# RMS norms of a two-block network on one core: first unit on unnormalized chunks, squares summed over chunks on VectorE, two norms in one pass

## What is computed

```python
def rms_norm(x, g, eps=NORM_EPS):
    xf = x.astype(jnp.float32)
    y = xf * lax.rsqrt(jnp.mean(xf * xf, axis=-1, keepdims=True) + eps)
    return (y * g.astype(jnp.float32)).astype(x.dtype)
```

## Time and profile before

| | |
|---|---|
| runs before | 2290.65, 2292.4, 2299.65 us; median 2292.4 |
| span of the profiled execution | 2289.6 us |
| the profiled execution's own time | not on the page; the median of the runs is 2.8 us above the span |
| TensorE matmul busy | 2172.8 us, 95% of the span |
| VectorE, ScalarE busy | 515.9 us (23%), 445.0 us (19%) |
| mean granted TensorE clock | 0.976 |
| memory traffic | 564 MB, 246 GB/s over the span |

### The profile page before, as it was taken

One profiled execution on the slowest core, in us unless ns is written; L12 is line 12 of the kernel. 1 busy time (PEld: TensorE's weight loads), 2 busy tenths in 40 slices (PEclk: granted clock), 3 DMA queues, 4 the chain that ended last, 5 costly groups with the idle time before them and its releaser, 6 DMA issues.

```text
span 2289.6 us, 27419 instructions
## 1 busy us (share of the span) xinstructions
PE 2172.8 (95%) x10542; PEld 1477.0 (65%) x10543; DVE 515.9 (23%) x1139; ACT 445.0 (19%) x794; POOL 6.9 (0%) x23
## 2 busy tenths in 40 slices
PE   8999989999999999999999899899999997999999
PEld 7686744444454444444444577678888886878887
DVE  3442111111121111111111128211000196110000
ACT  3342122222221221222222212221000123220000
POOL 0000000000000000000000000000000000000000
PEclk9999999999999999999999799999999998999999
DMA  7332679999999997999999633323444330324420
GB/s 298 124 134 92 241 298 422 422 422 422 422 371 356 422 402 299 421 422 422 422 422 422 249 111 111 146 75 147 155 158 147 128 130 32 116 74 147 149 90 19
DMA packets 78590, 564.36 MB, mean 246 GB/s; under 512 B 8864, under 2 KB 9248, under 8 KB 10176
## 3 DMA queue, kind: packets, MB, share of 16 engines
q1 hardware_dynamic: 77328, 554.94, 60.9%
q0 software_dynamic: 1200, 8.52, 0.9%
HBM read 558.19 MB, written 5.24 MB: 246 GB/s over the span
## 4 chain that ended last, share of the span: by engine, by line
PE 89%; DVE 5%; ACT 4%; issue 1%; DMA 0%; DVEq 0%; ACTq 0%; SPq 0%
PE bank L398 30%; PE bank L677 18%; PE bank L694 9%; PE bank L953 7%; PE bank L652 5%; DVE B L1775 3%; PE bank L704 3%; PE bank L520 2%; PE bank L726 2%; ACT B L997 2%; PE bank L408 2%; PE bank L745 1%; PE bank L664 1%; PE bank L643 1%; PE bank L903 1%
## 5 line engine op out<-in xcount | busy, mean ns | idle before, releaser
L398 PE MATMUL bank<-xn,ring 128*128 128x256 f32 x2560 | 574.2, 386 | 4.7 <-DVE xn L1338 4.7
L398 PEld LDWEIGHTS bank<-xn,ring 128*128 128x128 f32 x2560 | 495.5, 194 | 78.4 <-issue 9.2
L677 PE MATMUL bank<-ring,B 128*64 128x512 f32 x1920 | 418.6, 594 | 2.2 <-issue 2.2
L997 ACT ACTIVATE B<-bank 128x512 f32<-128x512 f32 (+3 forms) x293 | 150.0, 533 | 1279.2 <-PE bank L398 470.6
L677 PEld LDWEIGHTS bank<-ring,B 128*64 128x64 f32 x1920 | 135.5, 137 | 262.6 <-issue 259.0
L694 PE MATMUL bank<-ring,B 128*64 128x512 f32 x960 | 212.6, 595 | 0.0
L953 PE MATMUL bank<-B,ring 128*128 128x256 f32 x704 | 155.2, 379 | 0.0
L694 PEld LDWEIGHTS bank<-ring,B 128*64 128x64 f32 x960 | 66.3, 137 | 123.5 <-issue 119.9
L953 PEld LDWEIGHTS bank<-B,ring 128*128 128x128 f32 x704 | 133.8, 190 | 18.2
L652 PE MATMUL bank<-B 128*128 128x128 f32 x1056 | 124.7, 277 | 0.0
L398 PE MATMUL bank<-B,ring 128*128 128x256 f32 x512 | 116.2, 387 | 8.0 <-DVE B L1801 6.1
(11 more groups left out here) (266 smaller groups left out, 1442.9 us busy)
## 6 DMA issues: line engine op xcount, KB each, us to landing
ring<-in_stream SPq DMA_DIRECT2D x524, 1024.0 KB, 10.2
mem_kv<-ring POOLq DMA_DIRECT2D x4, 1024.0 KB, 7.2
B<-mem_kv POOLq DMA_DIRECT2D x4, 1024.0 KB, 6.8
xT<-in_x SPq DMA_DIRECT2D x1, 1024.0 KB, 4.9
ring<-in_mem SPq DMA_DIRECT2D x1, 1024.0 KB, 17.4
out_y<-xT SPq DMA_DIRECT2D x4, 256.0 KB, 2.5
tab<-in_tables SPq DMA_DIRECT2D x1, 960.0 KB, 10.6
tab<-in_tables SPq DMA_DIRECT2D x1, 544.0 KB, 11.5
```

Of the source, the lines that this page charges most:

```text
L398: mm = pe.matmul(dst[:, m, :], tile(u, m * C + k), rhs[:, k, :], start=(k == 0), stop=(k == C - 1))
L677: mm = pe.matmul(PS[4 + kind][NARROW * h:NARROW * (h + 1), :], xs[:, k, NARROW * h:NARROW * (h + 1)], ring[:, expert_slot(j), D * kk + 512 ...
L997: return act.activation(out_, in_, fn, **kw)
```

## The change

1. **Gains.** VectorE multiplies each residual chunk by the norm's gain alone into a new tensor xg, directly behind the residual add of its pair (gains).
2. **First unit on xg.** The first unit after a norm runs on xg instead of xn. Its output lacks the factor of each token; VectorE multiplies it in when it takes the bank out of PSUM (scale_first), into a new tensor un (or the tensor that ScalarE copied to before). The units behind the first still read xn, which is now xg x rb (normalize), two chunks in one operation, where rb is a copy of the spread in SBUF (copy_spread, ScalarE).
3. **Squares.** VectorE adds the pairs of squares into the first pair (add_squares, three operations of 128x512). TensorE then sums over the partitions with 4 matmuls (stat) instead of 16, placed inside the first unit behind its eighth matmul; the spread stands in front of its last one.
4. **Router.** Router and transposes read xg; the token's factor is applied by VectorE on the logits and by ScalarE on the token rows.
5. **Two norms in one pass.** For final and mix0 the product of both gains is applied at once. VectorE also sums squares weighted by the square of the final gain (in un); two more matmuls give the second mean of squares, from which the second factor is computed on 128x2 values. xT is multiplied by the final factor later, behind the scaling of the first units.
6. **Feed-forward ends.** The last down unit signals each bank (down_mm), and the residual adds start while it runs.
7. **Small ones.** Cross attention's query units use banks 0 and 1. Some semaphores are merged. The descriptor scratch of GpSimd's DMAs is set to 4096 (dynamic_dma_scratch_size).

The norms count 0 to 7 afterwards. The core of the diff:

```diff
@@ TensorE
-            def stationary(u, dst, rhs, ready=None):
+            def stationary(u, dst, rhs, ready=None, after=None):
...
-                            pe.wait_ge(ready[0], ready[1] + k + 1)
+                            pe.wait_ge(ready[0], ready[1] + k // ready[2] + 1)
...
+                        if after is not None and (m, k) in after:
+                            after[m, k]()
...
-                for c in (2 * j, 2 * j + 1):
+            def stat(n):
+                pe.wait_ge(S["ssum_ready"], n + 1)
+                for b in range(2):
+                    for c in range(2):
+                        mm = pe.matmul(PS[stat_bank(n)][:, b:b + 1], sq[:, c, b * P:(b + 1) * P], tb("ones")[:, 0:1],
+                                       start=(c == 0), stop=(c == 1))
+                if n == 2:
...
+                        mm = pe.matmul(PS[stat_bank(n)][:, 2 + b:3 + b], un[:, 0, b * P:(b + 1) * P],
+                                       tb("ones")[:, 0:1], start=True, stop=True)
+                mm.then_inc(S["stat_mm"], 1)
+            def spread(n):
+                pe.wait_ge(S["std_ready"], DEVS[n] + (4 if n == 2 else 2))
...
+            def first_unit(n, u, dst):
+                stationary(u, dst, xg, gained(n), {(0, 7): lambda: stat(n), (1, 6): lambda: spread(n)})
...
                 for j in range(4):
                     stationary(first + j, two(j), rhs, ready if j == 0 else None)
-                    if j and n is not None:
-                        stat_pair(n, j - 1)
-                if n is not None:
-                    stat_pair(n, 3)
...
-            for j in range(4):
-                stat_pair(0, j)
-            stationary(AT["lru_x"], two(0), xn, (S["xn_ready"], 0))
+            stationary(AT["lru_x"], two(0), xg, gained(0))
+            stat(0)
+            stationary(AT["lru_x"] + 1, two(1), xg, None, {(0, 7): lambda: spread(0)})
...
+            stat(1)
             for g in range(4):
...
-                                      xn[:, 4 * (g % 2) + c, (g // 2) * P:(g // 2 + 1) * P], tb("ident"))
+                                      xg[:, 4 * (g % 2) + c, (g // 2) * P:(g // 2 + 1) * P], tb("ident"))
...
-            for n in (2, 3):
-                for j in range(4):
-                    stat_pair(n, j)
-            for j in range(4):
-                stationary(AT["iq"] + j, two(j), xn, (S["xn_ready"], 24) if j == 0 else None)
+            stationary(AT["iq"], two(0), xg, gained(2), {(0, 7): lambda: stat(2)})
+            stationary(AT["iq"] + 1, two(1), xg, None, {(0, 1): lambda: spread(2)})
+            for j in range(2, 4):
+                stationary(AT["iq"] + j, two(j), xn, normed(2) if j == 2 else None)
...
+                    if g == NG - 1 and m % 2 and m < C - 1:
+                        mm.then_inc(S["down_mm"], 1)
...
@@ ScalarE
+            def copy_spread(n):
+                act.wait_ge(S["stat_mm"], STATS[n] + 2)
+                f(rb[:, :], PS[7 if n == 2 else stat_bank(n)][:, 0:T], ACT.Copy).then_inc(S["rb_ready"], 1)
...
-            for j in range(2):
-                act.wait_ge(S["units_done"], j + 1)
-                f(lxp[:, 2 * j:2 * j + 2, 2:2 + T], two(j), ACT.Copy).then_inc(S["lx_ready"], 1)
...
+            act.wait_ge(S["std_ready"], DEVS[1] + 2)
             for g in range(4):
                 act.wait_ge(S["tok_mm"], g + 1)
-                f(xtok[:, g // 2, 512 * (g % 2):512 * (g % 2) + 512], PS[6 + g % 2][:, :], ACT.Copy)\
+                f(xtok[:, g // 2, 512 * (g % 2):512 * (g % 2) + 512], PS[6 + g % 2][:, :], ACT.Identity,
+                  scale=nst[:, g // 2:g // 2 + 1])\
...
-            norm(2, "eps5")
-            norm(3)
+                squares(2, j)
+            deviation(2, "eps5")
+            act.wait_ge(S["std_ready"], DEVS[2] + 2)
+            f(nst2[:, :], nst2[:, :], ACT.Sqrt, scale=1.0 / D, bias=V("eps6")).then_inc(S["std_ready"], 1)
+            copy_spread(2)
...
@@ VectorE
+            def gains(n, j, gain):
...
+                for c in (2 * j, 2 * j + 1):
+                    g = gfm[:, c:c + 1] if n == 2 else V(gain, c)
+                    ts(xg[:, c, :], xT[:, c, :], g, None, ALU.mult).then_inc(S["xg_ready"], 1)
+            def add_squares(n, j):
+                dve.wait_ge(S["sq_ready"], 4 * n + j + 1)
+                settle()
+                if n == 2:
+                    for c in (2 * j, 2 * j + 1):
+                        if c == 0:
+                            link(ts(un[:, 0, :], sq[:, 0, :], gf2[:, 0:1], None, ALU.mult))
+                        else:
+                            link(stt(un[:, 0, :], sq[:, c, :], gf2[:, c:c + 1], un[:, 0, :], ALU.mult, ALU.add))
+                if j:
+                    o = tt(sq[:, 0:2, :], sq[:, 0:2, :], sq[:, 2 * j:2 * j + 2, :], ALU.add)
...
-                    stt(dst[:, k, :], xT[:, k, :], V(gain, k), PS[stat_bank(n)][:, 0:T], ALU.mult, ALU.mult)\
+            def normalize(n):
+                dve.wait_ge(S["xg_ready"], C * n + C)
+                dve.wait_ge(S["rb_ready"], SCALED[n] + 1)
+                for j in range(4):
+                    tt(xn[:, 2 * j:2 * j + 2, :], xg[:, 2 * j:2 * j + 2, :], over(rb[:, :], 2), ALU.mult)\
                         .then_inc(S["xn_ready"], 1)
-            def residual(first):
+            def scale_first(u, bank, dst, done):
+                dve.wait_ge(S["units_done"], u + 1)
+                tt(dst, two(bank), over(rb[:, :], 2), ALU.mult).then_inc(done, 1)
+            def norm(n, gain, u, bank):
+                rescale(n)
+                scale_first(u, bank, un[:, :, :], S["un_ready"])
+            def residual(first, n, gain):
                 for j in range(4):
                     dve.wait_ge(S["units_done"], first + j + 1)
                     tt(xT[:, 2 * j:2 * j + 2, :], two(j), xT[:, 2 * j:2 * j + 2, :], ALU.add)\
                         .then_inc(S["res_ready"], 1)
+                    gains(n, j, gain)
+                    add_squares(n, j)
...
-                dve.wait_ge(S["units_done"], AT[f"ffn{l}"] + 3 * NG)
                 for j in range(4):
+                    if j < 3:
+                        dve.wait_ge(S["down_mm"], 3 * l + j + 1)
+                    else:
+                        dve.wait_ge(S["units_done"], AT[f"ffn{l}"] + 3 * NG)
                     tt(xT[:, 2 * j:2 * j + 2, :], two(j), xT[:, 2 * j:2 * j + 2, :], ALU.add)\
                         .then_inc(S["res_ready"], 1)
+                    if l == 0:
+                        gains(5, j, "mix1")
+                        add_squares(5, j)
```

More of the change, by code:

```diff
@@ L929, in ffn @@
             def ffn(l):
[L930 removed]
+                first, n = AT[f"ffn{l}"], cross_norm(l) + 1
                 at = [first]
@@ L941, in ffn @@
                 down(l, NG - 1, at)
-                if l == 0:
-                    for j in range(4):
-                        stat_pair(6, j)
             def down(l, g, at):
@@ L1319, in _ @@
                 f(sq[:, c, :], hc[:, c, :], ACT.Sigmoid, bias=V("ln_b", c)).then_inc(S["lnsig_ready"], 1)
+            norm(6)
+            cross(1)
             norm(7)
-            cross(1)
-            norm(8)
             ffn(1)
@@ L1386, in _ @@
             dve.wait_ge(S["x_loaded"], 48)
+            for j in range(4):
+                gains(0, j, "norm1")
+            for j in range(4):
+                add_squares(0, j)
+            mark(tt(gfm[:, :], V("final", 0, C), V("mix0", 0, C), ALU.mult))
+            mark(tt(gf2[:, :], V("final", 0, C), V("final", 0, C), ALU.mult))
             ea, rate_n, rate_p = small[:, 16:24], small[:, 8:16], small[:, 24:32]
@@ L1393, in _ @@
             ts(ea, ea, -1.0, None, ALU.mult).then_inc(S["lam_exp"], 1)
-            norm(0, "norm1", xn)
+            rescale(0)
+            dve.wait_ge(S["pads_ready"], 3)
+            for j in range(2):
+                scale_first(AT["lru_x"] + j, j, lxp[:, 2 * j:2 * j + 2, 2:2 + T], S["lx_ready"])
             dve.wait_ge(S["act_chain"], 1)
@@ L1517, in _ @@
                     ALU.mult, ALU.mult).then_inc(S["mixed_ready"], 1)
-            residual(AT["w_out"])
-            norm(1, "norm2", xn)
+            residual(AT["w_out"], 1, "norm2")
+            dve.wait_ge(S["std_ready"], DEVS[1] + 1)
+            dve.reciprocal(nst[:, :], nst[:, :]).then_inc(S["std_ready"], 1)
+            dve.wait_ge(S["std_ready"], DEVS[1] + 2)
             dve.wait_ge(S["rout_mm"], 1)
             dve.wait_ge(S["pads_ready"], 6)
-            tt(lg[:, :, 0:E], PS[5][:, 0:2 * E].rearrange("p (a e) -> p a e", a=2), over(br[:, :], 2), ALU.add)\
+            mark(stt(lg[:, 0, 0:E], PS[5][:, 0:E], nst[:, 0:1], br[:, :], ALU.mult, ALU.add))
+            stt(lg[:, 1, 0:E], PS[5][:, E:2 * E], nst[:, 1:2], br[:, :], ALU.mult, ALU.add)\
                 .then_inc(S["lg_ready"], 1)
+            settle()
             dve.wait_ge(S["lg_ready"], 1)
@@ L1638, in _ @@
                                  n * STEPS_G + first.n, n * STEPS2)
-            norm(2, "final", xT)
-            norm(3, "mix0", xn)
```

(20 more changed lines are left out.)

174 lines of the change are left out of this document (110 added, 64 removed).

## The result

The changed kernel takes 2232.0 us (median of four runs, 2228.7 to 2236.7) against 2292.6 for the kernel before: ratio 0.9737, 95% interval 0.9717 to 0.9757, so 60.6 us or 2.6% less. The forecast was 2223, with 2215 to 2230 as its own range and 2238 as the end of the range that takes in rivals 1 to 4. The profiled execution is the slowest of the four: its time is 2236.7 and its span 2235.0, 54.6 us under the span of 2289.6 before.

What follows compares the result with a forecast made beforehand. TensorE, busy 95% of the span, was taken as the bound. Savings of 69.7 us off the 2289.6 span, plus 2.8 from span to median, gave 2222.7, stated as 2223; own range 2215 to 2230, extended to 2238 for rivals 1 to 4.

Steps and rivals of the forecast that it cites:

- rivals 1 to 4: Clock falls despite overlap (2236, 0.12); low over router transposes (2226, 0.05); first-unit waits bite (2237, 0.11); experts give gains back (2236, 0.05).
- The new course of a norm: From the last unit before a norm to its second unit's end: 16.1 us, including a 0.8 us TensorE wait.
- Gains: In each norm, VectorE makes two gained chunks at 0.41 us each, priced from a row with two operations.
- Router: Norm before the router: 6.1 us saved through the residual's reload, plus 1.8 for groups between units, 7.8 together.
- rival 2: Router stage: clock stays low over the transposes and the reload starts low, 3.5 us lost, 2226; chance 0.05.
- Merged norm: One pass for two norms after the experts: four units end 32.5 us after the bias matmuls, saving 18.2 us.
- Convolution's norm: Norm before the convolution: residual adds start inside the last down unit, chunks and sum just in time; 9.3 us saved.
- Rivals 1, 3, 5 and 6: Clock falls despite overlap (2236, 0.12); first-unit waits (2237, 0.11); expert weight shortage (2305, 0.02); early start not real (2256, 0.04).
- Start: Kernel start: first weights land at 9.1 us, two units end at 26.3 instead of 32.4; 6.0 us saved.
- The loop over the 32 experts is hardly touched: Loop over experts: one narrow expert keeps TensorE 28.3 of 29.23 us busy at full clock; DMA engines full too.
- Rival 4: Experts give back 13.8 us won before them, the weight queue falling 0.6 us behind each time; 2236, chance 0.05.
- Clock 1.00 throughout: Sign in each norm: first unit starts at once, second some 0.8 us after it, with TensorE's clock at 1.00.

## Why the prediction was right, point by point

- **The sum.** Forecast 69.7 us, measured 54.6 in the profiled execution and 60.6 in the medians. Its terms gave 70.5, within 2%; the two losses of the table, 15.7, and 0.2 of small steps make the 54.6.
- **The range held by luck in part.** 2232.0 is above the forecast's own range (2215 to 2230). It lies inside the stated range only because that was stretched to 2238 for rivals 1 to 4, and none of the four happened at its price; what took the time back was in no rival.
- **The new course of a norm** was right row by row: sum 0.79, root and reciprocal under the next chunks, a stand of 0.9 us where 0.8 was forecast. From the end of the last unit before it to the end of its second unit the first cross attention's norm took 16.3 us (forecast 16.1). That stand is an effect of where the spread was put: with it 1.3 us sooner the small vectors were ready too, and it went.
- **Gains** cost 0.35 us and not 0.41. The row taken had two operations.
- **Router.** Forecast 6.1, measured 6.3. The router ran warm (32 instructions in 3.63 us, 0.11 each, against 7.04 before), the sums too (0.87, not 1.75); the reload took 4.16 instead of 3.46, so rival 2 (a low clock over the transposes and into the reload) came to 0.7 of its 3.5 us.
- **Merged norm.** 18.2 and 19.0. **Convolution's norm** 9.3 and 9.1: the tight margins held. Rivals 1, 3, 5 and 6 did not happen: in every first unit behind chunks that were ready the chain passes through TensorE alone, and the experts' period is 29.22.
- **Start** 5.3 instead of 6.0. The cover of the q units held; the first weights landed at 9.21, not 9.1, and the rest is in the units, which start cold.
- **The smaller scratch of GpSimd's DMAs** was priced at 0; no run takes it back alone, so what it costs or gives is not shown.
- **The step that failed** is "The loop over the 32 experts is hardly touched", with "the experts' period stays 29.2" as its test: the period did stay, and 8.5 us were lost at its second round. Rival 4 had the experts give time back (13.8) for a wrong cause: the weights were there. The cause is the place of the loop in TensorE's program, which is 442 instructions shorter in all, 104 of them ahead of the loop; that the loop now closes before the next block of instructions has been asked for is the reading above.
- **"Clock 1.00 throughout"** held in the five later norms and failed in the mixed attention, which I had not read for what a shift does to it: 7.2 us in this profile, 2.9 of them by chance from run to run. The clock there goes with the time at which the stage starts, as far as the runs go: the index projection took 4.3 to 4.4 us in the five profiles in which it starts between 1321.9 and 1322.7, and 3.48 in seven that start at 1321.3 or after 1323.4, whatever the edit (3.90 in one more, at 1327.1). Why is open, and no run sets that time alone.

## What to carry to other kernels

A normalization whose scale is one number per token need not stand ahead of a linear unit: run the unit on the gained activations and scale its result, and put sum, root and spread inside that unit, early enough that each is ready when asked for. Add the squares on an idle engine first: sixteen one-column matmuls in place of four cost 2.7 us a norm here where TensorE's clock kept up, and 4.4 to 6.0 where it fell, though TensorE never stood. And after any edit of an engine's code ahead of a short loop, look at the first two rounds for "issue" time: a change of a hundred instructions moved a stand of 5.7 us and 2.8 us of low clock in or out.

The best kernel measured is the changed one with the spread after chunk 3: 2225.1 us, 0.9712 of the kernel before. With a cheaper way to move the loop (fewer and quicker instructions, or code moved from behind it), it would be some 8 us less by my estimate (the 5.6 us of the stand and the 2.6 of low clock behind it); that was not tried.

## What the runs showed that I had not expected

- A loop's second round on TensorE stands for 5.4 to 6.0 us in eleven profiles of programs with the loop's head at instruction 2,379, and not at all with it at 2,477, 2,479 or 2,483.
- Empty instructions vanish in compiling; 100 semaphore increments on TensorE took at most 0.15 us each.
- One-column matmuls: 0.10 us each for 8; 32 in a row took 0.14 us each in one norm, with 14 full-size instructions behind them in 5.36 us instead of 3.13 and TensorE busy throughout, and 0.11 each with 3.13 behind them in another.
- The index projection (32 instructions of 16 columns, then a chain of small VectorE steps) took 3.48 or 4.3 to 4.4 us, and the next unit 6.92 or up to 8.9. The two do not always go together: with no overlap in the merged norm the projection was warm (3.48) and the unit behind it took 8.91.
